# Each of the inverse's steps as two calls of 16 products, with large products between them

## What is computed

```python
def _gated_delta_rule(q, k, v, beta, g):
    ...
    lhs = eye + jnp.einsum("nbhik,nbhjk->nbhij", kb, k) * decay * (1.0 - eye)
    solve = functools.partial(lax.linalg.triangular_solve, left_side=True, lower=True,
                              unit_diagonal=True)
    u = solve(lhs, v * beta[..., None])
    w = solve(lhs, kb * jnp.exp(gc)[..., None])
    attn = jnp.einsum("nbhik,nbhjk->nbhij", q, k) * decay
    ...

def _gdn_mixer(x, w_in, conv_w, a_log, dt_bias, norm_w, w_out):
    qkv, z, ab = jnp.split(x @ w_in, [GDN_CONV_CH, GDN_CONV_CH + GDN_VAL_WIDTH], axis=-1)
    qkv = jax.nn.silu(_dwconv(qkv, conv_w))
    ...
    o = (_gated_delta_rule(q, k, v, beta[:, :, 0], g[:, :, 0])
         + _rev(_gated_delta_rule(_rev(q), _rev(k), _rev(v), _rev(beta[:, :, 1]), _rev(g[:, :, 1]))))
    o = _rms(o) * norm_w.astype(F32) * jax.nn.silu(z)
    return o @ w_out
```

## Time and profile before

| | |
|---|---|
| median of 3 runs | 1014.94 us (1012.57 to 1015.05) |
| the profiled execution | 1013.98 us, span of its instructions 1012.6 us |
| TensorE matmuls busy | 965.2 us, 95% of the span, 9305 records |
| TensorE weight loads busy | 754.5 us, 75% |
| VectorE busy | 556.6 us, 55% |
| ScalarE busy | 329.3 us, 33% |
| chain that ended last | TensorE 83% of the span, SP's queue 5%, VectorE 4%, DMA 4% |

### The profile page before, as it was taken

The page is one execution under the profiler, slowest core; times in us unless marked ns, Lnnn a source line. Parts: engine busy times, 40 slices in busy tenths (PEclk is TensorE's granted clock), DMA queues, the critical chain, the costliest instruction groups (busy, mean ns, idle before and its releaser), DMA issues.

```text
span 1012.6 us, 21917 instructions
## 1 busy us (share of the span) xinstructions
PE 965.2 (95%) x9305; PEld 754.5 (75%) x9305; DVE 556.6 (55%) x1192; ACT 329.3 (33%) x872; POOL 52.7 (5%) x81
## 2 busy tenths in 40 slices
PE   9999999999999999799876899999999999999999
PEld 6788888888888894344432588988888988877887
DVE  3976876876868243011100586875655465184675
ACT  2455556446545221001100322132121331233550
POOL 1111011011000000000000000000000000024000
PEclk9999999999999999799988999999999999999999
DMA  8213214134147999999999934442555344652221
GB/s 340 92 64 131 103 65 168 65 118 190 52 158 285 422 395 362 420 430 429 432 427 412 414 127 148 169 172 84 180 185 177 139 167 166 185 191 84 83 83 43
DMA packets 33622, 211.62 MB, mean 209 GB/s; under 512 B 4384, under 2 KB 8928, under 8 KB 15088
## 3 DMA queue, kind: packets, MB, share of 16 engines
q1 hardware_dynamic: 33520, 210.16, 53.9%
HBM read 209.03 MB, written 1.11 MB: 208 GB/s over the span
## 4 chain that ended last, share of the span: by engine, by line
PE 83%; SPq 5%; DVE 4%; DMA 4%; issue 2%; ACT 2%; DVEq 0%; ACTq 0%
PE ps L559 11%; PE ps L3159 9%; PE ps L3059 5%; PE ps L585 5%; SPq L1909 4%; PE ps L2023 4%; PE ps L3830 3%; PE ps L3799 3%; PE ps L3928 2%; PE ps L2668 2%; PE ps L1994 2%; PE ps L969 2%; PE ps L2063 2%; PE ps L805 2%; PE ps L3199 2%; PE ps L2905 2%
## 5 line engine op out<-in xcount | busy, mean ns | idle before, releaser
L559 PE MATMUL ps<-xt,slots 128*128 128x256 f32 x512 | 122.3, 384 | 0.0
L559 PEld LDWEIGHTS ps<-xt,slots 128*128 128x128 f32 x512 | 93.8, 190 | 12.8 <-issue 0.4
L1301 DVE SCALAR_TENSOR_TENSOR arena<-arena 128x256 f32<-128x256 f32 x128 | 56.6, 500 | 0.0
L2023 PE MATMUL ps<-arena 128*32 128x512 f32 x224 | 45.3, 622 | 7.1 <-DMA arena<-in_w 6.1
L2363 DVE TENSOR_TENSOR arena<-arena,ps 128x256 f32<-128x256 f32 x8 | 3.4, 422 | 84.1 <-ACT arena L2153 84.1
L4331 POOL TENSOR_TENSOR arena<-arena 128x512 f32<-128x512 f32 (+1 forms) x8 | 17.9, 2263 | 597.9 <-DVE arena L4139 597.9
L2023 PE MATMUL ps<-slots,arena 128*32 128x512 f32 x192 | 45.1, 613 | 1.0 <-DMA xt<-in_wu 0.8
L2153 ACT ACTIVATE arena<-ps 128x256 f32<-128x256 f32 x8 | 3.1, 385 | 107.7 <-PE ps L2023 107.7
L1994 PE MATMUL ps<-arena,x 128*128 128x128 f32 x256 | 32.0, 285 | 0.0
L1994 PEld LDWEIGHTS ps<-arena,x 128*128 128x128 f32 x256 | 30.9, 200 | 1.3 <-issue 0.8
L2023 PEld LDWEIGHTS ps<-arena 128*32 128x32 f32 x224 | 11.6, 115 | 26.8 <-issue 19.7
(11 more groups left out here) (589 smaller groups left out, 2177.9 us busy)
## 6 DMA issues: line engine op xcount, KB each, us to landing
slots<-in_wu SPq DMA_DIRECT2D x91, 1024.0 KB, 5.9
arena<-in_wu SPq DMA_DIRECT2D x20, 1024.0 KB, 14.2
arena<-in_w SPq DMA_DIRECT2D x5, 4096.0 KB, 25.6
slots<-in_w SPq DMA_DIRECT2D x8, 2048.0 KB, 30.7
extra<-in_w SPq DMA_DIRECT2D x2, 4096.0 KB, 26.1
yt<-in_w SPq DMA_DIRECT2D x3, 2048.0 KB, 27.2
extra<-in_wu SPq DMA_DIRECT2D x4, 1024.0 KB, 19.9
xt<-in_wu SPq DMA_DIRECT2D x4, 1024.0 KB, 28.6
```

Source lines behind the costliest of these rows:

```text
L559: q = M.matmul(bank(b, T), self.slots[:, s, k, n * P:(n + 1) * P], self.xt[:, k, :], start=(k == 0), stop=(k == KT - 1))
L1301: q = V.scalar_tensor_tensor(g.cn[:, s], src, w, g.cn[:, s], ALU.mult, ALU.add)
L2023: q = M.matmul(self.ps[r, 2, :], g.xg[:, half * (KT // 2) + k, r], self.flat(slots[e])[:, k * 512:(k + 1) * 512], start=(half == 0 and k = ...
```

## The change

The three step functions take a parameter `half` and issue 16 of the 32 products; the waits stand in the first half, the semaphore in the second. `project_half` and `z_product` take the parts to issue, so that they can be cut in two as well (two products each). In the main loop each step is called twice. Between the halves stands, from head 1 on, in the first round `solve` (first step), `attend` (second step) and `read_queries` (third step); in the second round half of a projection (first step), `solve` (second step) and `attend` (third step). All of these stood behind the whole step before. In head 0, where nothing of an earlier head is there, only the second round's first step has something between its halves. In head 7 the piece between the halves of the second round's first step is a whole `out_product`, and nothing stands behind the second half.

```diff
--- before.py
+++ after.py
@@ -541,7 +541,7 @@
         upto, behind = (c[n].rearrange("p (d i) -> p d i", d=2) for n in ("upto", "behind"))
         tile = lambda cc: slice(cc * P, (cc + 1) * P)
 
-        def project_half(h, j, part):
+        def project_half(h, j, part, two=(0, 1)):
             n = j % 2
             s = g.home(h, j // 2)
             group = (("qk", "v")[j // 2], h, n)
@@ -550,24 +550,27 @@
                 M.wait_ge(*g.first_in(1))
             if part == 1 and (h, j) == (0, 0):
                 M.wait_ge(*self.arrived[s](1))
-            if part == 0:
+            if part == 0 and 0 in two:
                 if (h, j) != (0, 0):
                     M.wait_ge(*self.landing(s))
                 if group in g.emptied:
                     M.wait_ge(*g.emptied[group])
-            for k in range(4 * part, 4 * part + 4):
+            for k in range(4 * part + 2 * two[0], 4 * part + 2 * two[-1] + 2):
                 q = M.matmul(bank(b, T), self.slots[:, s, k, n * P:(n + 1) * P], self.xt[:, k, :],
                              start=(k == 0), stop=(k == KT - 1))
-            if part == 1:
+            if part == 1 and 1 in two:
                 q.then_inc(*(self.multiplied[s] if n == 1 else (g.q_done, g.v0_done)[j // 2]).up())
 
-        def z_product(p, m):
+        def z_product(p, m, parts=(0, 1)):
 
             HK, xt, b = KT // 2, self.xt, g.banks["z", p, m]
             one, two = self.slots[:, 2], self.slots[:, 4]
             t1, t2, t4 = g.z_mixes
-            M.wait_ge(*g.emptied["z", p, m])
-            if m == 0:
+            if 0 in parts:
+                M.wait_ge(*g.emptied["z", p, m])
+            if 0 not in parts:
+                pass
+            elif m == 0:
                 M.wait_ge(*self.arrived[2](p + 1))
             elif m == 1:
                 M.wait_ge(*g.z_rows_made(4))
@@ -581,46 +584,53 @@
             rows, weights = ((xt[:, 0:HK, 0:P], one[:, 0:HK]), (g.z_rows[:, 1], t2), (g.z_rows[:, 2], two[:, 0:HK]),
                              (g.z_rows[:, 0], t1), (xt[:, HK:KT, 0:P], one[:, HK:KT]), (xt[:, HK:KT, P:2 * P], t4),
                              (g.z_rows[:, 3], two[:, HK:KT]))[m]
-            for k in range(HK):
+            for k in range(2 * parts[0], 2 * parts[-1] + 2):
                 q = M.matmul(bank(b, UC), rows[:, k, :], weights[:, k, :], start=(k == 0), stop=(k == HK - 1))
-            q.then_inc(*(self.multiplied[2] if m == 5 else self.multiplied[4] if m == 6 else g.z_products).up())
-
-        def first_step(h, k):
-
-            M.wait_ge(*g.x_made(3 * h + k))
-            M.wait_ge(*g.masked(2 * h + k))
-            for z in range(4):
+            if 1 in parts:
+                q.then_inc(*(self.multiplied[2] if m == 5 else self.multiplied[4] if m == 6 else g.z_products).up())
+
+        def first_step(h, k, half):
+
+            if half == 0:
+                M.wait_ge(*g.x_made(3 * h + k))
+                M.wait_ge(*g.masked(2 * h + k))
+            for z in (2 * half, 2 * half + 1):
                 at = slice(32 * z, 32 * z + 32)
                 for n, p in enumerate(hq):
                     M.matmul(ps[hq[n ^ 2], 3, at], g.mt[p, 0, z], g.X[p, 0, z], start=True, stop=True,
                              skip_group_check=True)
                     q = M.matmul(ps[p, g.ys_bank(k), at], g.mt[p, 1, z], g.X[p, 1, z], start=True, stop=True,
                                  skip_group_check=True)
-            q.then_inc(*g.ys.up())
-
-        def second_step(h, k):
-
-            M.wait_ge(*g.f_made(2 * h + k))
-            if k == 1 and h > 0:
-                M.wait_ge(*g.w_joined(h))
-            M.wait_ge(*g.w_moved(2 * h + k))
-            for z in range(4):
+            if half == 1:
+                q.then_inc(*g.ys.up())
+
+        def second_step(h, k, half):
+
+            if half == 0:
+                M.wait_ge(*g.f_made(2 * h + k))
+                if k == 1 and h > 0:
+                    M.wait_ge(*g.w_joined(h))
+                M.wait_ge(*g.w_moved(2 * h + k))
+            for z in (2 * half, 2 * half + 1):
                 for n, p in enumerate(hq):
                     M.matmul(g.twos_part(hq[n ^ 2], z), g.Y[p, 0, z], g.fw[p, 0:3:2, z], start=True, stop=True,
                              skip_group_check=True)
                     q = M.matmul(g.twos_part(p, 4 + z), g.Y[p, 1, z], g.fw[p, 0:2, 4 + z], start=True, stop=True,
                                  skip_group_check=True)
-            q.then_inc(*g.twos.up())
-
-        def third_step(h, k):
-
-            M.wait_ge(*g.v_made(4 * h + 2 * k))
-            for m in range(8):
+            if half == 1:
+                q.then_inc(*g.twos.up())
+
+        def third_step(h, k, half):
+
+            if half == 0:
+                M.wait_ge(*g.v_made(4 * h + 2 * k))
+            for m in range(4 * half, 4 * half + 4):
                 n = slice(m * 32, m * 32 + 32)
                 for p in hq:
                     q = M.matmul(ps[p, 3, n], g.T2[p, m // 4, m % 4], g.V[p, m // 4, m % 4], start=True, stop=True,
                                  skip_group_check=True)
-            q.then_inc(*g.thirds.up())
+            if half == 1:
+                q.then_inc(*g.thirds.up())
 
         def cross_y(h):
 
@@ -860,15 +870,15 @@
         for h in range(QKH):
             step, ahead, next_half = h > 0, h + 1 < QKH, h + 2 < QKH
 
-            def beside(n):
+            def beside(n, parts=(0, 1)):
 
                 if ahead and n < 4:
-                    project_half(h, 2 + n // 2, n % 2)
+                    project_half(h, 2 + n // 2, n % 2, parts)
                 elif ahead:
-                    z_product(h // 2, 4 * (h % 2) + n - 4)
+                    z_product(h // 2, 4 * (h % 2) + n - 4, parts)
                 elif n < 3:
-                    z_product(h // 2, 4 + n)
-                else:
+                    z_product(h // 2, 4 + n, parts)
+                elif 0 in parts:
                     out_product(*g.out_order[n - 3])
 
             def beyond(n):
@@ -880,38 +890,44 @@
                 else:
                     out_product(*((0, 6), (0, 7), (0, 5), (0, 4))[n])
 
-            first_step(h, 1)
+            late = h % 2
+            first_step(h, 1, 0)
             if step:
                 solve(h - 1, 0)
-                beside(0)
-            else:
-                beside(1)
-            second_step(h, 1)
+            first_step(h, 1, 1)
+            beside(0 if step else 1)
+            second_step(h, 1, 0)
             if step:
                 attend(h - 1, 0)
+            second_step(h, 1, 1)
+            if step:
                 read_keys(h - 1)
             beside(1 if step else 2)
-            third_step(h, 1)
+            third_step(h, 1, 0)
             if step:
                 read_queries(h - 1)
-            late = h % 2
+            third_step(h, 1, 1)
             if step:
                 beside(2)
             if not late:
                 beside(3)
-            first_step(h, 2)
+            first_step(h, 2, 0)
+            beside(4 - late, (0,))
+            first_step(h, 2, 1)
             if ahead and step:
                 unit_sums(h + 1)
-            beside(4 - late)
-            second_step(h, 2)
+            beside(4 - late, (1,))
+            second_step(h, 2, 0)
             if step:
                 solve(h - 1, 1)
+            second_step(h, 2, 1)
             beside(5 - late)
-            third_step(h, 2)
+            third_step(h, 2, 0)
+            if step:
+                attend(h - 1, 1)
+            third_step(h, 2, 1)
             if ahead and not step:
                 unit_sums(h + 1)
-            if step:
-                attend(h - 1, 1)
             beside(6 - late)
             cross_y(h)
             beside(7 - late)
```

## The result

The changed kernel takes **1023.32 us** (median of 6 executions, 1021.87 to 1026.9). The ratio of the two is put at 1.0093, with a 95% interval of 1.0078 to 1.0109: **slower by 9.4 us** (7.9 to 11.0). This ratio is not the quotient of the two medians, which lie 11.0 us apart. The forecast was 1024.0 us, 9.0 more than before.

What follows compares the result with a forecast made beforehand. The prediction took TensorE's own work in the eight delta-rule heads as the bound. Own work +6.8 us and waits 2.2 us gave 1023.0 from the profiled 1013.98, 1023.9 against the median 1014.94, rounded 1024.0; range 1018 to 1031.

Steps and rivals of the forecast that it cites:

- own work: TensorE's own pieces in the eight heads: price of splits less gain of pace, +6.8 us.
- the waits: TensorE waiting on later signals: 0.8 in heads 1, 3, 5, 1.1 in head 7, 0.3 in head 0; 2.2 us.
- Pace: Inverse step calls: both halves run at the first half's pace, saving 0.24, 0.17 and 0.04 us in the three steps.
- the choice between two bounds: Split calls: slow stretch stays, nothing saved, or both halves run at the fast pace; the latter was taken.
- The rival of halves that stay slow: Inverse step calls: splitting saves no pace, 1030.7 us; chance 0.08.
- Change of form: TensorE going from large products to small and back: each split adds 0.31 us, 0.33 in a second step.
- The rival of a hidden change: Split calls on TensorE: small weight loads run under the last large product, pace saving stays, 1010.8 us; chance 0.08.
- A small call in under 0.25 us behind a large product: TensorE's timeline: a sign that the prediction is wrong; it forecast 0.31 us before each half, 0.20 behind 128-wide products.
- the copy that was named: VectorE's turned Y before the second round's second step: waits of 0.27 us in heads 1, 3, 5, 1.11 in head 7.
- nothing would be lost in the first round: Before its second step: no wait, as convolution taps already delay VectorE's copy of Y; otherwise up to 1.4 us.
- The rival of longer waits: Heads 1 to 6: VectorE's chains half a microsecond later than counted, once in each head, 1027 us; chance 0.10.
- The end: Expert weight loads behind the heads: the delay counts in full; rival of half swallowed by the weight stream, 1019.5, chance 0.04.

Runs made afterwards that it cites:

- the kernel cut in three: The changed kernel with 35 of its calls cut again into 8, 16 and 8 products between large products; +20.6 us (16.2 to 24.9) over the kernel before.
- second steps alone: Against the kernel before, only the second steps of the inverse split, first and third whole; +3.4 us (1.2 to 5.7).
- third steps alone: Against the kernel before, only the third steps of the inverse split, first and second whole; +7.8 us (5.6 to 9.9).

## Why the prediction was right

**The time: right, in part by luck.** The forecast of 1024.0 stood on 1014.94, the median of three executions; over six the kernel before has 1012.31, and 9.0 more than that is 1021.3. What was forecast well is the difference: 9.0 against 9.4 by the ratio and 9.6 in the stage (11.0 by the medians). Of it, own work was forecast too low by 0.7 and the waits are right.

**Pace: right.** The split calls start 32 records within 0.16, 0.24 and 0.26 us in every head, and no half has a slow part. This was the choice between two bounds, and the cross product of the earlier trace rows was the right row to go by. The rival of halves that stay slow falls with the same rows.

**Change of form: right, a little too small.** 0.31 ahead (0.20 behind 128-wide products), 0.12 to 0.14 behind (0.15 to 0.18 ahead of `solve` in the first round, whose second product then comes 0.03 sooner), and 0.31 to 0.32 us for one change by the kernel cut in three. The rival of a hidden change falls there too: the middle calls stand between large products with no semaphore to wait for, and pay in full. Net a split costs 0.09, 0.18 and 0.28, where 0.07, 0.16 and 0.27 were forecast. Each is 0.01 to 0.02 more, no more than the rounding of rows to 0.01 us can hide, but it counts 14 times: 14 x 0.55 = 7.7, less head 7's 0.2, is 7.5 of own work against 6.8. TensorE's busy time grew by 7.7; what is above the 7.5 is waiting that the modelled end of the record ahead covers, 0.07 in each of heads 1, 3 and 5.

Four points of its working do not hold as written, and none moves the sum. In a rival and in a bound it counts 43 changes of form, where its own account of head 7 leaves 42. The 32 products that would fill the queue are 32 records, that is 16 products. A small call in under 0.25 us behind a large product, one of its signs of being wrong, is there behind 128-wide products, where it forecast 0.20 itself; the sign can only mean 256-wide ones. And against the rival of a hidden change it sets the Trainium skill's rule on loads for another row group, as it quotes it; a product of 128x128 takes all rows, so whether that rule covers the small loads behind it these runs do not tell. They show that the first small load came with its first product, in the changed kernel too (143.15 and 143.16 in head 3, after 0.33 us without a load).

**Waits: right in place and size.** Heads 1, 3, 5 and 7 wait on the copy that was named; of the others only head 0 does, by 0.11 us from start to start (42.68 + 1.13 - 0.38 = 43.43 to 43.85, against 0.31). The forecast was 0.27 each and 1.11; the idle rows have 0.21 and 1.12, and from the last large start to the first small one it is 0.59 in head 3 against 0.31 without a wait, 0.28 more. Head 0's wait on the weight mix grew by 0.2 (0.65 to 0.86), and the head by 0.33, where 0.3 was forecast.

That nothing would be lost in the first round held as well, but not by the order that was named for it. The prediction let VectorE's taps keep the copy of Y back, so that a later Y would not matter. The rows of head 3 in the first round, before and after:

```profile
138.01 0.88 POOL L1733 TENSOR_TENSOR arena<-arena 128x256 f32<-128x256 f32 x1 [2.81 <-PE ps L597]
138.22 0.95 DVE L1301 SCALAR_TENSOR_TENSOR arena<-arena 128x256 f32<-128x256 f32 x1
...
140.61 0.88 DVE L1317 SCALAR_TENSOR_TENSOR arena<-arena 128x256 f32<-128x256 f32 x2
141.89 0.45 DVE L1372 STREAM_TRANSPOSE arena<-arena 128x256 f32<-128x256 f32 x1 [0.41 <-ACT arena L1030]
```

Before, a tap took 0.95 us beside GpSimd's mask, which waits for the first step's products (line 597) and not, as the text on the kernel before may be read, for the third step's. With the change the mask starts later, at 141.52, and the two taps of this line that stand ahead of the copy take 0.88 together, where they took 1.35. VectorE is done with them early and idles 0.41 for ScalarE's copy of Y. The turned copy starts 2.33 us after the step's first product (139.56), against 2.32 before (137.17): the same, with another engine as the limit.

The rival of longer waits asked for 0.5 us more in each of heads 1 to 6: they grew by 1.05 to 1.12 (even) and 1.32 to 1.39 (odd), as forecast.

**The end: right, within what can be told.** From the stage's end to the end of the span it is 704.2 us before (1012.6 - 308.42) and 703.0 with the change (1020.6 - 317.65). In the seven other kernels it is 703.2 to 706.0, and 704.1 in the one whose stage is 21 us longer: it does not shrink as the stage grows, so the weight stream swallows nothing that shows beyond this spread of 3 us. The wait that was named for this, of 12.3 us in the earlier trace rows, has its length still (line 1150 is line 1134 of before):

```profile
SPq L520 <- ACT arena L1150: 12.3, 1, 12.3
```

**What stays open.** Of the six other kernels that were timed, five lost more in time than in the stage, by 0.7 to 1.8 us, and one less, by 0.5. That is inside the intervals and inside the spread of what lies behind the stage; whether a part of it is real these runs do not tell. What holds TensorE up in head 4, and what makes a call's pace break behind 32 records, stays open as well.

## What to carry to other kernels

A run of small-tile products between large ones costs a price for the change of form, here 0.31 us for runs of 8, 16 and 32 products alike; a cut pays only if what it saves exceeds that. Here shorter calls gain at most 0.24 us by their pace, so every cut loses, and the step whose long call had the least to gain loses the most. When a step's signal is moved behind other work, look at the engine that takes it up: if its next operation has another one queued ahead of it, try moving that one back. Here this took away three waits of 0.28 us each, and no new one came.

## What was not expected of the hardware

The price of a change of form does not depend on the size of the small piece: 0.31 us for pieces of 8 as of 16 products. And the break of pace in a call comes as a hole at record 33, 0.08 us long in a first step of 48 records; with it the last 16 records take 0.27 us, more than the 32 ahead of them (0.16). In a second step the hole lies over records 33 and 34 (140.91, 140.94, 141.00), and in a third step no single one stands out. A cut 16 records beyond the break keeps most of the loss.

The time of a VectorE operation depends on what GpSimd does beside it. The tap of line 1301 in the first round takes 0.95 us in heads 0 to 6 of every kernel whose first step is whole there (before, second steps alone, third steps alone). In the six others, where GpSimd's mask has moved behind it, it takes 0.48; there 0.95 is left in head 0 alone, whose first step has nothing between its halves.
